# One expert stream through three layers, token tile by token tile, with the other tile's mixer in pieces beside it

## The reference, cut to what matters

```python
q = (xf @ w_q).reshape(N, 8, 2, 128)                       # 16 queries a token
s = einsum('nhpd,hpkd->nhpk', q, subkeys)                  # 2 x 128 scores a head
top_s, top_i = top_k(s, 16)
best_s, best_pos = top_k(all 16 x 16 sums, 16)             # 16 experts of 16384 a head
idx, g = ..., softmax(best_s)
act = gelu(einsum('nd,nhkd->nhk', xt, u_tab[idx]))         # a dot with each expert's row u
y = einsum('nhk,nhkd->nd', g * act, v_tab[idx])            # a weighted sum of their rows v
```

## Time and profile before

| | before |
|---|---|
| median of 3 runs | 2781.26 us (2777.39 to 2781.36) |
| profiled execution, its time | 2780.64 us |
| its span | 2778.8 us |
| PE / DVE / ACT / POOL busy | 82% / 60% / 31% / 31% |
| mean DMA rate over the span | 327 GB/s |
| gathers | 768, 805.36 MB |
| loads by SP | 101.06 MB |

### The profile page before, as it was taken

One profiled execution on the slowest core, in us unless ns is written; L12 is line 12 of the kernel. 1 busy time (PEld: TensorE's weight loads), 2 busy tenths in 40 slices (PEclk: granted clock), 3 DMA queues, 4 the chain that ended last, 5 costly groups with the idle time before them and its releaser, 6 DMA issues.

```text
span 2778.8 us, 25580 instructions
## 1 busy us (share of the span) xinstructions
PE 2291.0 (82%) x7846; PEld 1262.6 (45%) x7846; DVE 1667.8 (60%) x3913; ACT 851.9 (31%) x2568; POOL 857.8 (31%) x804
## 2 busy tenths in 40 slices
PE   7989898887787778998887788777888888777776
PEld 6879764443233224764443233224755444222222
DVE  2853236666766664256666776764426667677764
ACT  2132013332333332323332333332423333333332
POOL 0022004334444341005344444441004434444441
PEclk9999799999999999989999999999999999999999
DMA  4310139999999996429999999996239999999996
GB/s 178 130 67 9 39 133 416 421 421 421 421 421 421 421 421 260 140 82 401 421 421 422 421 421 421 421 421 274 96 106 356 421 421 421 421 421 421 421 421 276
DMA packets 141750, 908.03 MB, mean 327 GB/s; under 512 B 15760, under 2 KB 19104, under 8 KB 43184
## 3 DMA queue, kind: packets, MB, share of 16 engines
q0 software_dynamic: 110592, 805.36, 69.7%
q1 hardware_dynamic: 31024, 101.06, 10.4%
HBM read 905.30 MB, written 1.05 MB: 326 GB/s over the span
## 4 chain that ended last, share of the span: by engine, by line
DMA 56%; PE 31%; DVE 6%; ACT 4%; issue 3%; POOL 1%; DVEq 0%; POOLq 0%; ACTq 0%
DMA arena<-in_uv,idx 56%; PE bank L1558 9%; PE bank L343 6%; PE bank L730 5%; DVE arena L1501 3%; PE bank L577 1%; PE bank L713 1%; PE bank L359 1%; ACT arena L1532 1%; PE bank L1764 1%; PE bank L563 1%; PE bank L1339 1%; POOL arena L1575 1%; ACT arena L1520 0%; PE bank L537 0%
## 5 line engine op out<-in xcount | busy, mean ns | idle before, releaser
L1558 PE MATMUL bank<-arena 128*128 128x512 f32 x3072 | 1444.5, 615 | 403.7 <-ACT arena L1532 397.6
L1575 POOL DMA_INDIRECT arena<-in_uv,idx x768 | 823.0, 1072 | 1670.0 <-PE bank L1558 1043.6
L1558 PEld LDWEIGHTS bank<-arena 128*128 128x128 f32 x3072 | 564.3, 193 | 1208.5 <-ACT arena L1532 621.9
L1501 DVE CUSTOM_DVE_ANT_0 arena<-arena,h 128x1024 f32<-128x1024 f32 x512 | 627.6, 1226 | 413.0 <-DMA arena<-in_uv,idx 412.3
L1520 ACT ACTIVATE arena<-arena 128x2 f32<-128x2 f32 x384 | 78.2, 204 | 1312.1 <-DVE arena L1501 1312.0
L1501 DVE CUSTOM_DVE_ANT_0 arena<-arena 128x1024 f32<-128x1024 f32 x256 | 313.9, 1226 | 213.5 <-DMA arena<-in_uv,idx 213.3
L1532 ACT ACTIVATE arena<-const,arena 128x128 f32<-128x128 f32 x768 | 260.3, 386 | 0.0
L343 PE MATMUL bank<-xT,weights 128*128 128x256 f32 (+1 forms) x944 | 218.7, 394 | 0.9 <-ACT xT L778 0.9
L343 PEld LDWEIGHTS bank<-xT,weights 128*128 128x128 f32 x944 | 183.8, 196 | 33.1 <-issue 2.1
L1526 ACT ACTIVATE arena<-arena 128x1 f32<-128x1 f32 x768 | 184.8, 288 | 12.6
L359 PE MATMUL bank<-xT,weights 128*128 128x256 f32 x672 | 163.7, 379 | 0.0
(11 more groups left out here) (321 smaller groups left out, 1757.7 us busy)
## 6 DMA issues: line engine op xcount, KB each, us to landing
weights<-in_w_q SPq DMA_DIRECT2D x48, 512.0 KB, 7.8
weights<-in_w_in SPq DMA_DIRECT2D x38, 512.0 KB, 3.3
arena<-in_uv,idx POOLq DMA_INDIRECT x768, 23.7
weights<-in_a_fm SPq DMA_DIRECT2D x14, 512.0 KB, 3.4
rows<-in_rows SPq DMA_DIRECT2D x10, 512.0 KB, 4.7
weights<-in_w_o SPq DMA_DIRECT2D x8, 512.0 KB, 3.3
weights<-in_a_out SPq DMA_DIRECT2D x8, 512.0 KB, 3.3
weights<-in_b_fm SPq DMA_DIRECT2D x8, 512.0 KB, 3.8
```

The source lines that it names most:

```text
L1501: V.tensor_tensor_reduce(out=u, in0=u, in1=x[:, unit // PH, :], scale=1.0, scalar=0.0, op0=ALU.mult, op1=ALU.add, accum_out=dots[:, unit % ...
L1558: ins = nc.tensor.matmul(acc[:, :], diag[:, e % DIAGS, :], ring[:, e % RING, at:at + 512], start=first, stop=last)
L1575: nc.gpsimd.indirect_dma_start(out=ring[:, s, :], out_offset=None, in_=io[f"uv{n}"], in_offset=bass.IndirectOffsetOnAxis(ap=idx[:, unit % ...
```

## The change

The three layers' expert parts become one stream of 48 units in six windows of 64 slots: window w is layer w // 2, tile w % 2. While one tile's experts of a layer are streamed, the other tile gets its norm, its next mixer, the norm after that, and its queries and scores, cut into pieces that stand at numbered slots of the window (`base` is the window's first slot, and in the mixers `o` is `base - 1`). So in window w + 1 the work beside the stream prepares window w + 2. What this brings with it:

- The mixers work on one tile at a time, so matmuls have 128 columns and not 256, and each of the weight blocks of mixers two and three and of the queries of layers two and three is loaded twice, once a tile. `load_row` is called six times more.
- RING is 8 in place of 12, since the mixers' tiles now lie beside the ring. SLOTS stays 6.
- Queries of layers two and three come in groups of one, one, two, two and two heads. The keys and values of both memories are computed in window 0.
- Layer 1 up to the first gather is as before.

```diff
-RING = 12
+RING = 8
...
-        def plan_peer(n):
...
+        for i in range(NT):
+            block_of(("glr", i), io["a_glr"], P // 8 * KC)
+            for j in range(3):
+                block_of(("a_q", i, j), io["a_fm"][j])
+                block_of(("a_k", i, j), io["a_fm"][3 + j])
+            for kc in range(KC):
+                block_of(("a_v", i, kc), io["a_v"][kc], 768)
+            for j in range(2):
+                block_of(("a_qm", i, j), io["a_fm"][12 + j])
+            for j in range(6):
+                block_of(("a_r", i, j), io["a_fm"][6 + j])
+            for kc in OUT_ORDER:
+                block_of(("a_out", i, kc), io["a_out"][kc])
+            plan_queries(Q_GROUPS, 1, i)
...
+        def fm_part(pe, job, block, i):
+            fm_tile(pe, job, block, xT[:, :, cols_of(i)], P)
...
+        def stream_tensor(pe):
+            beside = Beside(beside_tensor(pe))
+            beside.run(-1)
+            for s in range(UNITS // PH * WINDOW):
+                if s and s % WINDOW == 0:
+                    pe.wait_ge(sem("peer_added"), 2 * (s // WINDOW))
+                for e in range(s * GROUP, (s + 1) * GROUP):
...
+                    ins.then_inc(sem("v_used"), 1)
+                beside.run(s)
...
+        def beside_tensor(pe):
+            yield from first_tensor(pe)
+            for w in range(4):
+                n, i = w // NT + 1, w % NT
+                yield from (gla_tensor, sb_tensor)[n - 1](pe, i, WINDOW * (w + 1))
+                yield from queries_tensor(pe, n, i, WINDOW * (w + 1))
...
+        def beside_vector(v):
+            for w in range(6):
+                n, i, base = w // NT + 1, w % NT, WINDOW * (w + 1)
+                yield base
+                peer_added(v, w)
+                if n > 1:
+                    yield base + 1
+                    mean(v, 2 * n - 1, i)
+                yield base + 2
+                variance(v, 2 * n - 1, i)
...
+                if n < 3:
+                    yield from (gla_vector, sb_vector)[n - 1](v, i, base)
+                    yield from mixed_vector(v, ("a_out", "b_out")[n - 1], n, i, base)
...
+        def queries_tensor(pe, n, i, base):
+
+            yield base + 45
+            fm_tensor(pe, 2 * n, i, h)
+            for lo, hi in Q_GROUPS:
+                for j in range(lo, hi):
+                    yield base + 47 + j
...
+                    fm_part(pe, ("q", n, i, j), ("w_q", n, i, j), i)
...
+        def sb_scalar(act, i, base):
...
+            def softplus(q):
+                act.wait_ge(sem("z_abs"), 3 * i + q + 1)
+                nc.scalar.activation(sb_view(lb, i), sb_view(lb, i), ACT.Exp).then_inc(sem("sb_exp"), 1)
+                act.wait_ge(sem("sb_exp"), 3 * i + q + 1)
+                nc.scalar.activation(sb_view(lb, i), sb_view(lb, i), ACT.Ln, bias=ones[:, 0:1]).then_inc(sem("sb_ln"), 1)
...
+            yield o + 20
+            plain(act, ("qm", 1, i, 0), qm[:, 0, :])
+            att_exp(0)
+            softplus(1)
...
+        def sb_vector(v, i, base):
...
+            yield o + 19
+            log_two(0)
+            negative_abs(1)
+            yield o + 21
+            masked(0)
+            softplus(1)
...
         def _(pe):
             one_tensor(pe)
-            for n, mixer in enumerate((two_tensor, three_tensor, None)):
-                peer_tensor(pe, n)
-                if mixer:
-                    enter_tensor(pe, n)
-                    mixer(pe)
+            stream_tensor(pe)
```

More of the change, by code:

```diff
@@ new lines, in stream_vector @@
+        def stream_vector(v):
+            V = nc.vector
+            ops = topk(v)
+            beside = Beside(beside_vector(v))
+            beside.run(-1)
+            for _ in range(TOPK_OPS):
+                next(ops)
+            ahead = 0
+            for unit in range(UNITS):
+                w = unit // PH
+                x = (xn if w < NT else h)[:, w % NT, :]
+                for kx in range(PK):
+                    e = unit * PK + kx
+                    u = ring[:, e % RING, 0:D]
+                    v.wait_ge(*slot_filled(e))
+                    V.tensor_tensor_reduce(out=u, in0=u, in1=x, scale=1.0, scalar=0.0, op0=ALU.mult, op1=ALU.add,
+                                           accum_out=dots[:, unit % 2, kx:kx + 1]).then_inc(sem("dots"), 1)
+                    more = min(2, AHEAD - ahead) if kx < PK - 1 else 0
+                    for _ in range(2 + more if kx < PK - 1 else 0):
+                        next(ops, None)
+                    ahead += more
+                    if kx % GROUP == GROUP - 1:
+                        beside.run(e // GROUP)
+            beside.run(UNITS * PK)
@@ L1705, in memory_norm_vector @@
-        def memory_norm_vector(v, n):
-            v.wait_ge(sem("mem_exp"), 8 * (n + 1))
-            nc.vector.reciprocal(small[:, 24:32], small[:, 24:32]).then_inc(sem("dve_step"), 1)
+            for par in range(2):
+                r = slice(64 * par, 64 * par + 64)
+                pe.wait_ge(*banks.take(("ms", n, i, par)))
+                out = banks.bank(("ms", n, i, par))
+                for j in range(2):
+                    ins = nc.tensor.matmul(out[:, j * 256:(j + 1) * 256], qm[r, j, :], mem_k[n][r, j, :],
+                                           start=True, stop=True)
+                ins.then_inc(banks.full_sem(("ms", n, i, par)), 1)
@@ new lines, in gla_scalar @@
+            yield o + 29
+            memory_out_scalar(act, 0, i)
+            for par in range(2):
+                yield o + 30 + par
+                act.wait_ge(*banks.full(("o2", i, par)))
+                out = banks.bank(("o2", i, par))
+                to = cat[:, 0:6, :].rearrange("p (j two) t -> p j two t", two=2)[:, :, par, :]
+                ins = nc.scalar.activation(to, out[:, 0:384].rearrange("p (a b) -> p a b", a=3), ACT.Copy)
+                ins.then_inc(banks.emptied_sem(("o2", i, par)), 1)
```

1723 lines of the change are left out of this document (932 added, 791 removed).

## The result

The changed kernel took 2656.8 us in the median of four runs (2655.4 to 2659.7), against 2780.8 of the kernel before on the same chip: a ratio of 0.956, 95% interval 0.954 to 0.958. The forecast was 2633 us, its range 2612 to 2700. So the change is 4.4% faster, and the forecast was 24 us, 0.9%, too low. The profiled execution is the one of 2659.7 us, with a span of 2657.9.

The account below looks back on a forecast made before the run. DMA was taken as the bound from 438 us on: 912.2 MB at 421 GB/s take 2167 us, last landing 2605, plus 16.6 of tail, 10 of lateness and 1.8 around the span: 2633 us, range 2612 to 2700.

Parts of the forecast that it names:

- The rate of the added loads: Loads beside the gathers: taken to run at 421 GB/s, with 350 kept for the range, costing 52 us more.
- Rival C: Loads beside the gathers run at 350 GB/s: 2685 us, sign a full DMA share at a lower rate; chance 0.09.
- PE, DVE, ACT in a window: Mixer windows: PE 329 us and DVE some 265 of 379; ACT adds one small copy a slot; all fit.
- the ring's sum: Gather ring of 8: round 19.9 us, 13.5 left for the DMA; in mixer windows 23.7 and 13.4, slack 6 to 7.
- The first 438 us: Layer one up to 438 us stays as before, with 47.3 MB moved by then at 108 GB/s.
- Lateness: Late slots in the mixer windows let the gather queue run dry: 10 us over all windows, up to 40 in the range.
- three places named: Window's start, mixer two's 5.0 us reciprocal, mixer three's crowded slots for tile 1: each may run the queue dry 0 to 5 us.
- the window's start: DVE waits for the last expert's matmul, some 2 us beyond its normal pace, and PE waits for DVE.
- D: Mixer windows slowed by PE's granted clock: loses below a mean grant of 0.79, 2873 us at 0.75; chance 0.05.
- A: Ring runs dry often in the four mixer windows: 58 us more, 2691 us; chance 0.15.
- forecast case: Whole kernel: 2612 to 2660 us, at a chance of 0.62.
- B: Activation table switches on ACT laid open: 40 x 1.28 = 51 us, 2684 us; chance 0.06.

Follow-up runs that it names:

- e11: Against the changed kernel: short norms, short reciprocal, copies for mixer three's Exp and Ln, and first query blocks ahead of SP's wait; 2648.4 us, 0.953 to 0.955.
- e1: Against the changed kernel: SP loads the blocks up to the memory's keys before waiting for the first norms; 2651.2 us, 0.952 to 0.956 of the kernel before.
- e5: Against the changed kernel: mixer two's reciprocal covers 128 of its 768 elements, so the output differs; 2661.5 us, 0.956 to 0.958 of the kernel before.
- e6: Against the changed kernel: mixer three's softplus Exp and Ln and attention Exp become copies, so the output differs; 2656.0 us, 0.954 to 0.957 of the kernel before.

## Why the prediction was nearly right, step by step

**What bounds it.** Right. The DMA share is 1.01 in the stream, the plateaus stand at 421 GB/s, the valleys are filled, and the bytes are right to 0.1 MB. Four windows of experts beside mixers take 383 to 386 us each, where 379 was worked out.

**The rate of the added loads.** Right to take 421. The stretch from 1060 to 1340 us has 280 us of mixers and queries beside the gathers and moved 421. Rival C, 350 GB/s for the loads, is refuted as a price. Its sign, a full share at a lower rate, does occur in small (405 GB/s at a share of 1.00 from 1780 to 1860 us), but it needs no loads: the last stretch of e11 has it without any.

**PE, DVE, ACT in a window.** A mixer window was to hold 329 us of PE and 265 of DVE in 379; from 779 to 1163 us it held 338 and 254 in 384. The engines fit, as said. The last gather's 13.5 us of landing are the 13.5 that the ring's sum has for a stream with nothing beside it.

**The first 438 us.** This step failed: "Layer one up to 438 us stays: the first queries, the first 30 steps of `topk` and the first gathers are the same instructions." They are the same instructions on PE, DVE, ACT and POOL. On SP a wait for the norms was put ahead of the query blocks that the first queries need. It cost 8.2 us until the first gather and 3.1 MB by 438 us, and e1 shows it. The description of the change, "Layer 1 up to the first gather is as before", has the same fault. The diff had the line; I counted what each step issues and did not read SP's queue in its order.

**Lateness.** The mechanism was right and the term too small: 10 us were taken, 29 were measured, 24 of them in four places. Some 15 of the 24 are gathers issued late, which is what the term was for; the other 9 are a lower rate at a busy DMA, for which the forecast had no term. Two of the three places named are there: the reciprocal of mixer two (4.95 us, as worked out, dips at 990 and 1380 us) and slot `o + 20` of mixer three for tile 1. The third, the window's start, cost next to nothing: 60 us over each window start moved 418 to 422. In its place there is the window's end of mixer three for tile 0 (3.0 us), where the residual, the norm and the softmax's Exp fall in neighbouring slots. That these make it is not shown: the short norms brought 405 to 417 there, but so did the spread values (419), which leave the norms alone.

The slot `o + 20` shows why a stall costs more than its length. ACT and then PE:

```profile
2058.60 1.28 ACT L2257 ACT_TABLE_LOAD   x1
2059.90 1.06 ACT L2257 ACTIVATE arena<-arena 128x1024 f32<-128x1024 f32 x1
2060.86 1.04 ACT L2249 ACTIVATE arena<-arena 128x1024 f32<-128x1024 f32 x1
2061.92 1.28 ACT L2251 ACT_TABLE_LOAD   x1
2063.22 1.15 ACT L2251 ACTIVATE arena<-arena,const 128x1024 f32<-128x1024 f32 x1
2064.38 1.28 ACT L1565 ACT_TABLE_LOAD   x1
2065.68 0.20 ACT L1565 ACTIVATE arena<-arena 128x2 f32<-128x2 f32 x1
```

```profile
2058.11 3.60 PE L1520 MATMUL bank<-arena 128*128 128x512 f32 x8
2061.54 1.95 PE L348 MATMUL bank<-xT,weights 128*128 128x128 f32 x16
2066.74 6.67 PE L1520 MATMUL bank<-arena 128*128 128x512 f32 x8 [3.25 <-ACT arena L1577]
```

Three loads and three passes make 7.1 us between the pair before and the Gelu; PE waits 3.25 us, as the forecast's "2 to 3 us late" has it. But then the eight matmuls (a slot's four of the program) take 6.67 us, not 3.60. The granted clock says why, from 2060 to 2080 us:

```profile
2060.00:2080.00 20.00, 16.75 (x50) 8.34 (x50) 17.04 (x39) 9.59 (x21) 6.98 (x6) 0.83 0.90 362
```

0.83 over 20 us means that a third of them were at the lower level of 1.2 GHz, and windows of 2 us place it: 0.98 while PE stands still, 0.50 from 2066 to 2072, 1.00 from 2074. So a wait of 3 us became a delay of 6. At 990 us, behind the reciprocal, it is similar and milder: PE waits 6.35 us, the clock is 0.73 and 0.59 in the two windows of 5 us from 985, and sixteen matmuls take 8.86 us, not some 7.3. The forecast had the clock only as a rival for whole windows (D), which is refuted (0.96 to 0.98 in the four windows; the 0.97 or more that the forecast named as a sign was just missed over the whole execution, 0.966). As an amplifier of single stalls it was missing from the lateness term. The Trainium skill (ScalarE: Activation LUTs, What ACT_TABLE_LOAD costs) counts a drain of 1.38 us beside each load; here the Exp starts 1.30 us after the load's start, 1.28 of it the load, so the measurement decides against a drain in these rows.

**The rivals.** A, a ring that runs dry often, was priced at 58 us; what happened is its mild form, between the forecast case and A. B, table loads exposed everywhere, is refuted as a sum: most of them fall into ACT's idle time. At slot `o + 20` and `o + 25` they are exposed, and copies in place of the functions took up to 9 us of loss away there, without any gain in time. E did not occur.

**What stays open.** The lateness does not add up from its places. The reciprocal's slots and slot `o + 20` answer to their edits, in the windows where they stand; the kernel's time does not. Two theories fell on this, that the single late slots set the loss and that DVE's norms do. What the windows show is that loss appears elsewhere: partly as a new dip at the next crowded slots (e5), partly as a lower rate at a full DMA share (e6, e11). What sets the second, and how much of it varies from one execution to the next, these runs can't tell; one profile of each kernel is too few for differences of 4 us, by which the executions of one kernel differ too. So of the 26 us by which the last gather lands too late, 7 are explained by SP's order, and the cause of the 19 of lateness is shown only in part.

## What to carry to other kernels

When a change writes out an in-order queue anew, read every queue around the place, the one that only issues loads above all: a wait moved ahead of a load that others need costs its landing, here 8 us until the first gather beside a gain of 124. When work is put beside a stream of transfers, the sum by bytes gives a floor that is nearly reached, and the late slots a term of some 1%; don't expect to win them back one by one: here no repair of a single place brought time. Before a dip in a rate is repaired, ask whether the DMA share fell with it. If it did, gathers were issued late; if not, late issue is not what the dip shows, and another cause has to be looked for. And before a window of one profile is read as a gain, look how far kernels that do the same there differ.

## What the runs showed of the hardware

- After an idle of 3.25 us PE needed 6.67 us for eight matmuls of 512 columns that take 3.6 to 3.7 otherwise, at a granted clock of 0.50 for most of them.
- On ACT a copy of 1024 elements took 1.05 us and an Exp 1.04 to 1.06; a table load took 1.28.
- Gathers and loads together moved 421 GB/s, as gathers alone, over stretches of 280 us. At a DMA share of 1.00 to 1.01 the rate was 402 to 421 over stretches of 80 to 280 us, with the right gathered rows and with others: the share alone doesn't tell that the rate is at its full level.
